# The norm behind w_o moves onto scores and expert blocks, and picks of four heads are decoded between router heads

## Chip, cores, metric

The kernel runs on one core of a Trainium2 chip. The metric is the device time of one execution in microseconds (us); the time before is the median of three runs.

## The reference, cut to what matters

Two transformer blocks follow each other. The change lies in the second, between its mixing output and its mixture of experts (256 tokens, width 2048, 8 heads, 128 keys per half, 16 picks of 16384 experts per head):

```python
x = x + mixed @ w_o[l]
x = x + peer(rmsnorm(x, norm_ffn_g[l]), peer_wq[l], keys1, keys2, peer_u[l], peer_v[l])

def peer(x, wq, keys1, keys2, u, v):
    q = (xf @ wq).reshape(t, PEER_HEADS, PEER_QDIM)
    s1 = jnp.einsum('thd,kd->thk', q[..., :half], keys1)
    s2 = jnp.einsum('thd,kd->thk', q[..., half:], keys2)
    v1, i1 = lax.top_k(s1, 16)
    v2, i2 = lax.top_k(s2, 16)
    cand_s = (v1[..., :, None] + v2[..., None, :]).reshape(t, PEER_HEADS, -1)
    top_s, pos = lax.top_k(cand_s, 16)
    expert = ...                                # from i1, i2 and pos
    gate = softmax(top_s)
    z = xc . u[expert]
    out = (gelu(z) * gate) @ v[expert]
```

rmsnorm divides each token's row by its root mean square and multiplies column k by a gain.

## The kernel before, in words

The kernel streams all weights once from memory, in units of 128x1024 floats (512 KB) through a ring of four slots of `raw`; SyncE (SP) loads slot n again as soon as DVE's split of it is done (`lo_ready`). A unit is split in two reduced-precision parts: ScalarE (ACT) writes `w_hi` (`split_hi`, L495), VectorE (DVE) `w_lo = raw - w_hi` (`split_lo`, L504). `ahead(...)` in an engine's program is such a split for the pair of units two pairs further on; it waits until TensorE (PE) has finished the unit four before. Activations are split likewise into `act_hi` and `act_lo`. Every engine's program is written out by hand in the order in which it runs; semaphores join them.

In `w_o`, PE runs blocks of 96 matmuls (`mix_block`, `tokens_out`, L601 to L603) for 512 columns of both halves of 128 tokens; DVE adds the banks to X (`add_blocks`), ACT squares the sum (`block_squares`). Then comes the norm: DVE adds the last bank (`add_last`, L1937), ACT squares and takes the root, DVE the reciprocal; X is scaled to XN (L1953, L1115), PE transposes it (`turn_ffn`, L2590, 32 of 128x128), ACT and DVE keep `act_hi` (`keep_ffn_hi`, L1121) and `act_lo` (`keep_ffn_lo`, L1959), 16 chunks of 128x256 each.

The router stage has 8 turns, one a head, of four blocks each: two query blocks and two expert blocks (`u`, the first 16 of 128). A block is two units of `halves_out`: 8 matmuls of 512 columns with `w_hi` (L561) and 8 of 256 with `w_lo` (L568). GpSimd (POOL) adds the two halves of a block that ACT copied (`add_copied`, L729). PE forms scores (L2620), ACT keeps them (`keep_scores`, L1160), DVE takes the top 16 of each half (`top16`, L1985 to L1993) and of the 256 candidates (L2011). In a turn DVE runs: splits of pair 0, of pair 1, top 16, of pair 2, top 16, of pair 3, candidates. ACT puts expert blocks through gelu and stores them (`save_early`).

In the decode stage PE goes on with 16 expert blocks in banks 2 and 3 (`decode_turn`; it waits for the addition two blocks back), ACT keeps the low half (`low_half`, L574), DVE adds the other (`add_halves`, L579), ACT puts gelu in place and stores the block (L1195, L1197). Between them DVE decodes the picks of all 8 heads: conversion of positions (L2040 to L2045), then for two index sets and two halves of the heads a comparison with 0 to 15 (L2053), a product with the indices (L2062) and a reduction (L2067); `more()` puts a weight split and, each second time, an addition in between. Then 80 blocks follow in which the gate table is built and scattered, 16 late blocks, and the product with `v`.

## Time and profile before

| | us |
|---|---|
| median of three runs (2696.03 to 2696.39) | 2696.3 |
| the profiled execution | 2696.89 |
| span of its trace | 2695.2 |
| PE busy | 2669.4 |
| DVE busy | 1835.3 |
| ACT busy | 1369.4 |
| POOL busy | 371.4 |

The span runs from the first to the last recorded instruction; the profiled execution's own time is 1.7 us longer. A busy PE is one with a matmul in flight, which is not PE at its peak: matmuls overlap, and a matmul of 512 columns that shows 0.39 us follows its forerunner after 0.23. In a timeline the number in front is the start, then the duration; what stands in brackets is the idle time of the engine before it and what ended it. Here PE has work for almost the whole span, so what matters is where it waits.

### The profile page before, as it was taken

To read this page: it belongs to the slowest core of one execution; us is meant where nothing else is said; L and a number is where in the kernel's file an instruction comes from. 1 tells how busy PE (TensorE), PEld (TensorE's weight loads), DVE (VectorE), ACT (ScalarE), POOL (GpSimd) and SP (SyncE) were. 2 spreads that over 40 slices of the span, in tenths; PEclk is the share of its full clock that TensorE was granted. 3 is DMA by queue.
4 is the path that set the end of the run, shared out by engine and by line. 5 is a ranking of instruction groups with operands and counts; after the bars stand their busy time and mean duration, and the time that the engine had idled before them with its cause. 6 is when DMAs were issued, how large, how long until landed. Compare 5 with 4: busy or idle time off the path is not lost.

```text
span 2695.2 us, 47112 instructions
## 1 busy us (share of the span) xinstructions
PE 2669.4 (99%) x14299; PEld 2298.4 (85%) x14299; DVE 1835.3 (68%) x2985; ACT 1369.4 (51%) x2066; POOL 371.4 (14%) x296
## 2 busy tenths in 40 slices
PE   8999999999999999999999999999999999999998
PEld 6888888898888998888888888888888888888887
DVE  6666665668987677489996777775565555555555
ACT  6454445555665444455455555554444444444444
POOL 0010000001011211011105555551000000000000
PEclk9999999999999999999999999999999999999999
DMA  7566555564554554655567777777976666666564
GB/s 257 189 216 213 181 199 177 177 219 159 172 176 156 167 168 157 195 201 186 195 201 212 202 202 203 201 204 218 305 240 217 217 217 219 212 220 216 200 241 156
DMA packets 204475, 543.26 MB, mean 202 GB/s; under 512 B 37504, under 2 KB 82816, under 8 KB 203392
## 3 DMA queue, kind: packets, MB, share of 16 engines
q1 hardware_dynamic: 148112, 486.74, 54.9%
q10 hardware_dynamic: 35568, 47.33, 5.0%
q0 software_dynamic: 20736, 8.46, 2.7%
q8 instruction: 30, 0.49, 0.1%
q14 instruction: 29, 0.24, 0.0%
HBM read 515.12 MB, written 27.33 MB: 201 GB/s over the span
## 4 chain that ended last, share of the span: by engine, by line
PE 94%; DVE 3%; ACT 1%; issue 1%; DMA 0%; SPq 0%; DVEq 0%; POOL 0%; ACTq 0%; POOLq 0%
PE bank L561 32%; PE bank L568 16%; PE bank L2693 8%; PE bank L2694 8%; PE bank L2695 8%; PE bank L601 4%; PE bank L603 4%; PE bank L602 4%; PE bank L2488 1%; DVE w_lo L504 1%; PE bank L527 1%; PE bank L528 1%; PE bank L529 1%; PE bank L2658 1%; PE bank L2465 0%
## 5 line engine op out<-in xcount | busy, mean ns | idle before, releaser
L504 DVE TENSOR_TENSOR w_lo<-raw,w_hi 128x1024 fp32r<-128x1024 f32 x902 | 1097.9, 1226 | 725.9 <-ACT w_hi L495 719.4
L495 ACT ACTIVATE w_hi<-raw 128x1024 fp32r<-128x1024 f32 x902 | 950.8, 1059 | 946.5 <-PE bank L568 363.1
L561 PE MATMUL bank<-act,w_hi 128*128 128x512 f32 x3840 | 975.2, 396 | 2.6 <-DVE cst L579 1.0
L561 PEld LDWEIGHTS bank<-act,w_hi 128*128 128x128 f32 x3840 | 692.0, 189 | 133.8 <-issue 6.4
L568 PEld LDWEIGHTS bank<-act,w_lo 128*128 128x128 f32 x3840 | 519.7, 190 | 33.1
L568 PE MATMUL bank<-act,w_lo 128*128 128x256 f32 x3840 | 535.6, 282 | 0.0
L2693 PE MATMUL bank<-w_hi,expert_act 128*128 128x512 f32 x1008 | 392.3, 389 | 0.1
L2694 PE MATMUL bank<-w_lo,expert_act 128*128 128x512 f32 x1008 | 392.2, 389 | 0.0
L2695 PE MATMUL bank<-w_hi,expert_act 128*128 128x512 f32 x1008 | 392.1, 389 | 0.0
L742 POOL DMA_INDIRECT g_kept<-slot_t x128 | 239.7, 1872 | 253.8 <-issue 170.4
L2693 PEld LDWEIGHTS bank<-w_hi,expert_act 128*128 128x128 f32 x1008 | 189.3, 188 | 39.6 <-DVE cst L579 0.5
L2695 PEld LDWEIGHTS bank<-w_hi,expert_act 128*128 128x128 f32 x1008 | 189.3, 188 | 39.3
L2694 PEld LDWEIGHTS bank<-w_lo,expert_act 128*128 128x128 f32 x1008 | 189.3, 188 | 39.1
L601 PE MATMUL bank<-w_hi,act 128*128 128x512 f32 x320 | 125.8, 393 | 2.0 <-DVE act L1401 1.1
L603 PE MATMUL bank<-w_hi,act 128*128 128x512 f32 x320 | 124.7, 390 | 0.0
L602 PE MATMUL bank<-w_lo,act 128*128 128x512 f32 x320 | 124.6, 389 | 0.0
L748 POOL TENSOR_TENSOR big<-big 128x1024 f32<-128x1024 f32 x2 | 5.8, 2878 | 839.4 <-DVE big L2196 839.4
L601 PEld LDWEIGHTS bank<-w_hi,act 128*128 128x128 f32 x320 | 60.1, 188 | 16.2 <-DVE w_lo L504 1.3
L603 PEld LDWEIGHTS bank<-w_hi,act 128*128 128x128 f32 x320 | 60.1, 188 | 12.6
L602 PEld LDWEIGHTS bank<-w_lo,act 128*128 128x128 f32 x320 | 60.1, 188 | 12.1
L729 POOL TENSOR_TENSOR big<-big 128x256 f32<-128x256 f32 x32 | 33.1, 1034 | 248.3 <-ACT big L1138 248.3
L2107 DVE SCALAR_TENSOR_TENSOR weighted<-cst,slot_t 128x256 fp32r<-128x256 f32 x128 | 61.3, 479 | 0.0
(344 smaller groups left out, 2498.4 us busy)
## 6 DMA issues: line engine op xcount, KB each, us to landing
raw<-in_stream SPq DMA_DIRECT2D x902, 512.0 KB
z_kept<-cst ACTq DMA_DIRECT2D x112, 128.0 KB, 2.4
cst<-z_kept ACTq DMA_DIRECT2D x112, 128.0 KB, 3.9
g_kept<-zeros POOLq DMA_DIRECT2D x16, 512.0 KB
big<-in_ukv ACTq DMA_DIRECT2D x16, 512.0 KB, 4.6
big<-g_kept SPq DMA_DIRECT2D x16, 512.0 KB, 5.6
big<-in_rows ACTq DMA_DIRECT2D x3, 1024.0 KB, 5.8
big<-in_x SPq DMA_DIRECT2D x2, 1024.0 KB, 10.2
```

Source lines behind the costliest of these rows:

```text
L495: act.activation(w_hi[:, s, :], raw[:, s, :], ACT.Copy).then_inc(hi_ready, 1)
L504: dve.tensor_tensor(w_lo[:, s, :], raw[:, s, :], w_hi[:, s, :].bitcast(F32), ALU.subtract).then_inc(lo_ready, 1)
L561: pe.matmul(bank[:, :], w_hi[:, s, kk * P:(kk + 1) * P], act2[:, k, :, :].rearrange("p a n -> p (a n)"), start=(k == 0), stop=False)
L568: mm = pe.matmul(bank[:, 0:S], w_lo[:, s, kk * P:(kk + 1) * P], act_hi[:, k, :], start=False, stop=(k == KT - 1))
L601: pe.matmul(outs[t], a_hi, hi, start=(k == 0), stop=False)
L602: pe.matmul(outs[t], a_hi, lo, start=False, stop=False)
L603: mm = pe.matmul(outs[t], a_lo, hi, start=False, stop=(k == KT - 1))
L742: pool.indirect_dma_start(g_kept, bass.IndirectOffsetOnAxis(ap=SLOT_INDEX[:, i:i + 1], axis=0), SLOT_GATE[:, i:i + 1], None, compute_op=AL ...
L2107: dve.scalar_tensor_tensor(out=weighted[:, tile, :, :], in0=iota.unsqueeze(1).broadcast_to([P, 2, P]), scalar=first_index[:, bass.ds(tok, 1)],
L2693: pe.matmul(o, a_hi, hi, start=first, stop=False, skip_group_check=True)
L2694: pe.matmul(o, a_hi, lo, start=False, stop=False, skip_group_check=True)
L2695: mm = pe.matmul(o, a_lo, hi, start=False, stop=False, skip_group_check=True)
```

## The change

It has three parts.

1. The norm. X goes untouched to the transposes. `turn_block` (the helper of the two earlier norms) transposes columns of blocks 0, 1, 2 in the middle of the next block of `w_o`, and of block 3 between the two units of the first query block. `keep_hi_tiles` and `keep_lo_tiles` make the tiles with the gain alone. The factor 1/rms of a token is put on later: on scores by `keep_scores` (two activations, a scale each); on expert blocks by a product with FFN_ROW, a row of 1/rms in all partitions, which PE makes of a matrix of ones and two diagonals. POOL multiplies the router stage's expert blocks, DVE all others (`scale_rows`), in front of gelu.
2. The picks of heads 0 to 3 are decoded in turns 2 to 7 of the router, two heads in three turns: one piece behind pair 0's splits, one behind pair 3's. In the decode stage heads 4 to 7 are left.
3. In the decode stage gelu writes to `Z_HALVES` instead of in place, and the wait for the store before last stands in front of gelu, no longer in front of the copy of the low half; the copy comes ahead of the gelu of the block before. The softmax's Exp comes after two turns, not four.

```diff
+            def early_block(n, block):
+                z = Z_HALVES[:, n, 0:S]
+                pool.wait_ge(copied, block + 5)
+                step(pool.tensor_tensor(z, z, Z_HALVES[:, n, S:2 * S], ALU.add))
+                pool.wait_ge(row_kept, 2)
+                step.wait()
+                pool.tensor_tensor(z, z, FFN_ROW, ALU.mult).then_inc(pool_summed, 1)
...
+            ahead(split_hi, act, "w_o", 0, 8, 15, units=(0,))
+            keep_hi_tiles(3, pa("ffn_gain"), act_hi, 3)
             ahead(split_hi, act, "w_o", 0, 8, 15, units=(1,))
-            keep_ffn_hi(range(8, 16))
...
-                    act.activation(PS[:, a, :, :].rearrange("p t n -> p (t n)"), banks[4 + a][:, 0:S],
-                                   ACT.Copy).then_inc(ps_kept[a], 1)
+                    for t in range(TT):
+                        kept = act.activation(PS[:, a, t, :], banks[4 + a][:, t * P:(t + 1) * P], ACT.Copy,
+                                              scale=rstd[:, t:t + 1])
+                    kept.then_inc(ps_kept[a], 1)
...
+            def save_decoded(i, n, last=False):
+                act.wait_ge(z_scaled, i * 2 + (n + 1))
+                act.wait_ge(z_saved[n % 2], i * 16 + (16 * (PH + n // 2) + 1))
+                dest = GZ[:, n % 2, :] if last else Z_HALVES[:, n % 2, 0:S]
+                act.activation(dest, GZ[:, n % 2, :], ACT.Gelu).then_inc(gelu_ready[n % 2], 1)
...
+                        if part == "w_o" and b and k == 1:
+                            keep_lo_tiles(4, pa("ffn_gain"), act_hi, act_lo, b - 1)
...
             add_last(0)
             mean_last(0)
             root_last(0)
-            dve.wait_ge(added[1], 8)
-            norm_last(0, 0)
             add_last(1)
-            for cc in range(1, 4):
-                norm_last(0, cc)
             mean_last(1)
             root_last(1)
-            dve.wait_ge(added[1], 9)
-            norm_last(1, 0)
-            norm_last(1, 1)
-            keep_ffn_lo(range(8))
             ahead(split_lo, dve, "w_o", 0, 8, 15, units=(0,))
-            keep_ffn_lo(range(8, 16))
+            keep_lo_tiles(4, pa("ffn_gain"), act_hi, act_lo, 3)
+            step(dve.memset(ONES, 1.0))
+            for t in range(TT):
+                step(dve.tensor_scalar(RSTD_DIAG[:, t, :], ident, rstd[:, t:t + 1], None, ALU.mult))
...
+            def early_picks(h, first):
+                lo = 2 * ((h - 2) // 3)
+                piece = 2 * ((h - 2) % 3) + (0 if first else 1)
+                a = piece // 3
+                if piece == 0:
+                    convert_picks(lo, lo + 2)
+                if piece % 3 == 0:
+                    compare_picks(a, lo, lo + 2)
+                elif piece % 3 == 1:
+                    step.wait()
+                    for head in range(lo, lo + 2):
+                        index_picks(a, head)
+                else:
+                    collect_picks(a, lo, lo + 2)
...
+            def scale_rows(n, block):
+                wait_summed(dve, block)
+                dve.tensor_tensor(GZ[:, n, :], GZ[:, n, :], FFN_ROW, ALU.mult).then_inc(z_scaled, 1)
...
-            mix_block(0, 1)
+            mix_block(0, 1, range(4))
+            turn_block(2, 0, added, 4)
+            mix_block(0, 1, range(4, 8))
...
+            def first_queries():
+                pe.wait_ge(copied, 1)
+                pe.wait_ge(added[1], 8)
+                pe.wait_ge(act_lo_ready, 4 * KT + 12)
+                halves_out(pe, pair_of("wqu", 0, 4, 0), odd_of("wqu", 0), banks[0], units=(0,))
+                turn_block(2, 3, added, 4)
+                halves_out(pe, pair_of("wqu", 0, 4, 0), odd_of("wqu", 0), banks[0], units=(1,), paced=4 * KT)
```

The order on DVE at the end of `w_o`, before (L1937 addition, L1941 to L1948 mean and reciprocal, L1953 scaling of X, L1959 `act_lo`, L504 weight split):

```order
L1937 TENSOR_TENSOR big<-big,bank 128x512
L1941 TENSOR_REDUCE stat<-stat 128x1
L1943 TENSOR_SCALAR stat<-stat 128x1
L1948 RECIPROCAL stat<-stat 128x1
L1953 TENSOR_SCALAR big<-big,stat 128x512
L1937 TENSOR_TENSOR big<-big,bank 128x512
L1953 TENSOR_SCALAR big<-big,stat 128x512 x3
L1941 TENSOR_REDUCE stat<-stat 128x1
L1943 TENSOR_SCALAR stat<-stat 128x1
L1948 RECIPROCAL stat<-stat 128x1
L1953 TENSOR_SCALAR big<-big,stat 128x512 x2
L1959 SCALAR_TENSOR_TENSOR act<-bank,par,act 128x256 x8
```

And now (line numbers of the changed kernel; L1941 addition, L1366 `act_lo`, L505 weight split):

```order
L1941 TENSOR_TENSOR big<-big,bank 128x512
L1945 TENSOR_REDUCE stat<-stat 128x1
L1947 TENSOR_SCALAR stat<-stat 128x1
L1952 RECIPROCAL stat<-stat 128x1
L1941 TENSOR_TENSOR big<-big,bank 128x512
L1945 TENSOR_REDUCE stat<-stat 128x1
L1947 TENSOR_SCALAR stat<-stat 128x1
L1952 RECIPROCAL stat<-stat 128x1
L505 TENSOR_TENSOR w_lo<-raw,w_hi 128x1024
L1366 SCALAR_TENSOR_TENSOR act<-bank,par,act 128x256 x4
L1964 MEMSET big 128x128
L1966 TENSOR_SCALAR big<-cst,stat 128x128 x2
```

The six scalings of X are gone, twelve of the sixteen `act_lo` tiles stand earlier in `w_o`, and the diagonals are new.

DVE in the router between turns 2 and 3, before (one of two candidate rounds, then the splits):

```order
L2011 TENSOR_TENSOR big<-big 128x256
L1985 MAX big<-big 128x8
L1987 MAX_INDEX big<-big 128x8
L1989 MATCH_REPLACE big<-big 128x256
L1991 MAX big<-big 128x8
L1993 MAX_INDEX big<-big 128x8
L504 TENSOR_TENSOR w_lo<-raw,w_hi 128x1024 x4
```

And now, with L2013 the reduction of `collect_picks`:

```order
L2051 TENSOR_TENSOR big<-big 128x256
L1974 MAX big<-big 128x8
L1976 MAX_INDEX big<-big 128x8
L1978 MATCH_REPLACE big<-big 128x256
L1980 MAX big<-big 128x8
L1982 MAX_INDEX big<-big 128x8
L505 TENSOR_TENSOR w_lo<-raw,w_hi 128x1024 x2
L2013 TENSOR_REDUCE big<-big 128x64
L505 TENSOR_TENSOR w_lo<-raw,w_hi 128x1024 x2
```

A piece of the decoding has come between the splits of pair 0 and pair 1; another one stands behind pair 3's splits, ahead of the next candidates.

PE at the start of the router, now (L2617 to L2619 end of `w_o`, L559 and L566 the two halves of a unit, L2287 transposes, L2652 the row of 1/rms, L2642 scores); before, all 32 transposes stood ahead of the first unit:

```order
L2619 MATMUL bank<-w_hi,mix_lo 128x512
L559 MATMUL bank<-act,w_hi 128x512 x8
L566 MATMUL bank<-act,w_lo 128x256 x8
L2287 MATMUL bank<-cst,big 128x128 x8
L559 MATMUL bank<-act,w_hi 128x512 x8
L566 MATMUL bank<-act,w_lo 128x256 x8
L559 MATMUL bank<-act,w_hi 128x512 x8
L566 MATMUL bank<-act,w_lo 128x256 x8
L559 MATMUL bank<-act,w_hi 128x512 x8
L566 MATMUL bank<-act,w_lo 128x256 x8
L2652 MATMUL bank<-big 128x128 x2
L2642 MATMUL bank<-big 128x128 x2
```

Only the last 8 transposes are left here, behind the first unit.

## Rows read from the trace of the kernel before

**Rows 1.** The page's busy line, then two stages: span, busy us of each engine, clock, DMA

```profile
PE 2669.4 (99%) x14299; PEld 2298.4 (85%) x14299; DVE 1835.3 (68%) x2985; ACT 1369.4 (51%) x2066; POOL 371.4 (14%) x296
...
1184.00:1361.00 177.00, 176.71 (x1032) 155.92 (x1031) 160.38 (x437) 90.66 (x124) 29.20 (x29) 1.00 0.57 188
1420.00:1880.00 460.00, 460.00 (x2676) 406.48 (x2675) 319.74 (x559) 242.76 (x388) 236.61 (x127) 1.00 0.74 205
```

**Rows 2.** Timeline of PE, end of w_o and start of the router's second block

```profile
1151.92 0.39 PE L2582 MATMUL bank<-w_hi,mix_lo 128*128 128x512 f32 x1
...
1166.20 2.00 PE L561 MATMUL bank<-act,w_hi 128*128 128x512 f32 x8
...
1169.00 2.00 PE L561 MATMUL bank<-act,w_hi 128*128 128x512 f32 x8
```

**Rows 3.** Timeline of PE, third decode block

```profile
1358.26 2.10 PE L561 MATMUL bank<-act,w_hi 128*128 128x512 f32 x8 [0.29 <-DVE cst L579]
```

**Rows 4.** Timeline of PE, transposes among matmuls in the stage of w_out

```profile
378.44 1.03 PE L2256 MATMUL bank<-cst,big 128*128 128x128 f32 x8
...
379.55 0.40 PE L602 MATMUL bank<-w_lo,act 128*128 128x512 f32 x1
```

**Rows 5.** Timeline of DVE and ACT at the end of w_o

```profile
1149.69 0.69 DVE L1937 TENSOR_TENSOR big<-big,bank 128x512 f32<-128x512 f32 x1 [0.41 <-PE bank L2582]
...
1151.66 1.04 ACT L495 ACTIVATE w_hi<-raw 128x1024 fp32r<-128x1024 f32 x1
...
1155.99 1.57 ACT L1121 ACTIVATE act<-bank,par 128x256 fp32r<-128x256 f32 x4 [0.30 <-PE bank L2590]
...
1156.87 1.66 DVE L1959 SCALAR_TENSOR_TENSOR act<-bank,par,act 128x256 fp32r<-128x256 f32 x4 [1.01 <-ACT act L1121]
```

**Rows 6.** Timeline of PE in the router, scores and the unit behind them

```profile
1334.56 0.61 PE L2620 MATMUL bank<-big 128*128 128x128 f32 x4
1334.93 2.09 PE L561 MATMUL bank<-act,w_hi 128*128 128x512 f32 x8
1336.86 0.99 PE L568 MATMUL bank<-act,w_lo 128*128 128x256 f32 x7
```

**Rows 7.** Timeline of DVE in the router, weight splits

```profile
1295.39 1.23 DVE L504 TENSOR_TENSOR w_lo<-raw,w_hi 128x1024 fp32r<-128x1024 f32 x1 [0.26 <-ACT w_hi L495]
...
1331.51 3.48 DVE L504 TENSOR_TENSOR w_lo<-raw,w_hi 128x1024 fp32r<-128x1024 f32 x3
1335.86 1.23 DVE L504 TENSOR_TENSOR w_lo<-raw,w_hi 128x1024 fp32r<-128x1024 f32 x1 [0.87 <-ACT w_hi L495]
```

**Rows 8.** Timeline of DVE at the start of decoding, and PE's fourth decode block

```profile
1357.70 0.42 DVE L579 TENSOR_TENSOR cst<-cst,bank 128x256 f32<-128x256 f32 x1
...
1359.24 2.40 DVE L504 TENSOR_TENSOR w_lo<-raw,w_hi 128x1024 fp32r<-128x1024 f32 x2
1361.56 0.41 DVE L579 TENSOR_TENSOR cst<-cst,bank 128x256 f32<-128x256 f32 x1
1361.89 2.28 DVE L2053 TENSOR_TENSOR big<-big,cst 128x2048 f32<-128x2048 f32 x1
...
1365.23 1.29 DVE L2062 TENSOR_TENSOR big<-big 128x512 f32<-128x512 f32 x2
...
1367.57 0.41 DVE L579 TENSOR_TENSOR cst<-cst,bank 128x256 f32<-128x256 f32 x1
...
1363.95 2.00 PE L561 MATMUL bank<-act,w_hi 128*128 128x512 f32 x8
```

**Rows 9.** Timeline of ACT in the loop behind the softmax's Exp

```profile
1396.22 1.28 ACT L495 ACT_TABLE_LOAD   x1
1397.51 1.06 ACT L495 ACTIVATE w_hi<-raw 128x1024 fp32r<-128x1024 f32 x1
```

**Rows 10.** By line, 1184 to 1361 us: duration ns min/median/max, first and last start

```profile
L504 DVE TENSOR_TENSOR w_lo<-raw,w_hi x62: 1203/1218/1227, 1183.8 to 1360.4; 128x1024 fp32r<-128x1024 f32 x62
L729 POOL TENSOR_TENSOR big<-big x29: 737/744/1297, 1188.1 to 1349.6; 128x256 f32<-128x256 f32 x29
```

More of the change, by code:

```diff
@@ L1168, in router_turn @@
                 keep_query(1)
+                if first:
+                    act.wait_ge(row_made, 2)
+                    act.activation(FFN_ROW, banks[6][:, 0:S], ACT.Copy).then_inc(row_kept, 1)
+                    act.wait_ge(rstd_ready, 7)
                 keep_scores(0)
@@ L1183, in early_turn @@
                     ahead(split_hi, act, "u_decode", i, 2, n, units=(0,))
+                    act.wait_ge(unit_done, 2 * pair_of("u_decode", i, 2, n) + 2)
+                    if first:
+                        act.wait_ge(z_saved[n], 16 * PH + 1)
+                    act.wait_ge(gelu_ready[n], i + (PH + 1))
+                    low_half(act, GZ[:, n, :], banks[2 + n])
+                    ahead(split_hi, act, "u_decode", i, 2, n, units=(1,))
                     if first and not n:
@@ L1228, in gates_turn @@
                     if gates:
+                        if first and not n:
+                            act.wait_ge(z_saved[0], 32 * PH + 1)
                         act.wait_ge(hot_used[2 * n + 1], i + 2)
@@ L1993, in top16, with convert_picks @@
                 return dve.max_index(idx[:, 8:16], vals[:, 8:16], work)
+            wide = TT * PK
+            def convert_picks(lo, hi):
+                cols = slice(lo * wide, hi * wide)
+                step.wait()
+                places = CP[:, lo:hi, :, :].rearrange("p h t k -> p (h t k)")
+                step(dve.tensor_scalar(CAU[:, 0, cols], places, 4, None, ALU.logical_shift_right))
+                step(dve.tensor_scalar(CAU[:, 1, cols], places, 15, None, ALU.bitwise_and))
+                step(dve.tensor_copy(I12F[:, lo:hi, :, :, :].rearrange("p h a t k -> p (h a t k)"),
+                                     I12[:, lo:hi, :, :, :].rearrange("p h a t k -> p (h a t k)")))
+                step.wait()
+                step(dve.tensor_copy(CA[:, :, cols], CAU[:, :, cols]))
@@ new lines, in compare_picks @@
+            def compare_picks(a, lo, hi):
+                step.wait()
+                step(dve.tensor_tensor(EQ[:, lo * wide * PK:hi * wide * PK].rearrange("p (n j) -> p n j", j=PK),
+                                       CA[:, a, lo * wide:hi * wide].unsqueeze(2)
+                                       .broadcast_to([P, (hi - lo) * wide, PK]),
+                                       iota[:, 0:PK].unsqueeze(1).broadcast_to([P, (hi - lo) * wide, PK]),
+                                       ALU.is_equal))
@@ L2023, in next_low @@
                     add_halves(dve, GZ[:, pair % 2, :], banks[2 + pair % 2], block_of("u_decode", 0, 2, pair))
+                    if not pair:
+                        dve.wait_ge(row_kept, 2)
+                    scale_rows(pair % 2, block_of("u_decode", 0, 2, pair))
             def more(count=1):
@@ L2037, in _ @@
             more(2)
[L2039 to L2045 removed]
+            half = PH // 2
@@ L2046, in _ @@
+            convert_picks(half, PH)
             more(2)
[L2047 to L2049 removed]
             for a in range(2):
[L2051 to L2070 removed]
@@ L2071, in _ @@
+                compare_picks(a, half, PH)
+                more()
+                step.wait()
+                for h in range(half, PH):
+                    index_picks(a, h)
+                    if h % 2:
+                        more()
+                collect_picks(a, half, PH)
+                more()
             dve.wait_ge(pick_exp, 1)
@@ L2624, in query_scores @@
                     halves_out(pe, pair_of("wqu", h, 4, 2 + a), odd_of("wqu", a), banks[2 + a])
-            queries_out(0, 0, paced=True)
+            first_queries()
             queries_out(0, 1)
+            pe.wait_ge(rstd_ready, 8)
+            for t in range(TT):
+                ins = pe.matmul(banks[6][:, t * P:(t + 1) * P], ONES, RSTD_DIAG[:, t, :], start=True, stop=True)
+            ins.then_inc(row_made, 1)
             pe.wait_ge(table_ready, 32)
```

149 lines of the change are left out of this document (44 added, 105 removed).

## Prediction, made blind

> **What bounds the kernel now.** I read the page first. TensorE (PE) is busy for 2669.4 us of the 2695.2 us span [rows 1], so a change can win only where PE waits, and can lose wherever a helper engine makes it wait. What to look for is therefore the few places where PE stands, and how near VectorE (DVE) is to being late elsewhere.
>
> The table by stage shows the second thing. In the router stage (1184 to 1361 us) PE has 176.71 of 177 us, and DVE 160.38: 91% [rows 1]. In the stage of the gate tables (1420 to 1880 us) DVE has 319.74 of 460 us, so it has room there.
>
> PE's timeline shows the first. The last w_o matmul starts at 1151.92; with 0.23 us each PE is through at 1152.15. The second router block starts at 1166.20 and a unit of sixteen matmuls lasts 2.80 us [rows 2]. So the first router block, two units or 5.60 us of work, took 14.05 us: **8.45 us** are the norm (32 transposes, square root, scaling) and its waits.
>
> The other place is where decoding starts: PE's third decode block begins at 1358.26 after a wait for DVE's addition (L579) [rows 3]. That addition frees the bank, and in DVE's program it stands behind all weight splits (L504, w_lo) and all of the top-16 work before it. So at this point DVE is already the bound: what DVE is late by here, PE is late by too.
>
> **The change, part by part.**
>
> *The norm leaves the path.* Raw X is transposed inside w_o: 8 transposes start at 378.44 and the matmul after next at 379.55 [rows 4]; less one matmul of 0.23 that is 0.88 us for 8. 24 of them in w_o: 2.64 us on PE. Then the first router unit runs at once (2.80), then the last 8 transposes (0.88) and four matmuls of the second unit (0.92): 4.60 us after the w_o end, which I call T. Chunk 12 needs the tiles that ACT and DVE write. From the start of DVE's addition to ACT's first weight split are 1.97 us, 1149.69 to 1151.66 [rows 5]. The first half's matmuls end twelve matmuls before 1152.15, at 1149.42, and its addition starts 0.27 later; so for the second half the addition starts at T+0.27 and ACT at T+2.24. The split (1.04) ends at T+3.3, when the first transposed chunks are there too; ACT's four tiles (1.57, [rows 5]) follow it, DVE's split ends at T+4.5, and DVE's four tiles (1.66, [rows 5]) make the last at T+6.1. Then one matmul (0.23) and the low half (0.95): T+7.3. Against 14.05 that is 14.05 - 7.3 - 2.64 = 4.1 us less. The row of 1/rms (two small products, the form of L2620) costs 0.37 start to start and makes the next group 0.09 longer [rows 6], so 0.45. **Front: -3.65 us.** Bounds: if nothing waited, 8.45 - 3.52 - 0.45 = -4.5; with 0.8 us of handovers more, -2.9. The tiles of blocks 0 to 2 (12 x 0.4 us on ACT and on DVE) fall into w_o, whose blocks last 22 us; nothing for them.
>
> *Picks between router heads.* DVE gets, in turns 2 to 7, twice: a conversion, and for each of two index sets a comparison and a reduction 128x1024 and two products 128x512. DVE instructions overlap by 0.08: three splits of 1.22 take 3.48 [rows 7], 1.13 each. Comparison and reduction I take at 1.13 (same width as the split; the 2048-wide one is 2.28, twice that, [rows 8]), two products at 1.20 (1.29 less 0.08, [rows 8]). The conversion took 1.20 us for four heads' widths and more (1357.70 to 1359.24, less the addition's 0.33, [rows 8]); a quarter of the width, between 0.3 and 1.2, I take 0.7. Sum: 2 x (0.7 + 2 x 3.46) = 15.2 us in six turns.
>
> What DVE can give: it waits for ACT's w_hi once 0.87 and twice 0.26 us a turn [rows 7]; with the lost overlaps 3 x 0.08 that is 1.63 us, 9.8 in six turns. The rest is lateness: 1.4, 2.0, 2.7, 4.1, 4.7 us at the ends of turns 2 to 6 and **5.4 us** at the end of turn 7. Until turn 6 it is covered by the ring of four weight units: the tightest split ends at 1332.74 and PE uses it at 1336.86 [rows 6, 7], 4.1 us later. At the end all of it meets the addition that PE already waits for. **Router: +5.4 us**; bounds +4.6 (conversion 0.3) and +7.1 (conversion 1.2, no overlap at half of the pieces).
>
> *Decoding.* DVE's cycle from addition to addition is 6.01 us where picks are decoded, 1361.56 to 1367.57 [rows 8], against PE's 5.59. Before, eight such blocks lose 8 x 0.42, less 1.97 of lead (addition done 1361.98, PE starts 1363.95, [rows 8]): 1.4 us. Now four blocks are left, each with a scaling of 0.45 (0.41 as L579, behind it on the same data): 4 x 0.87 - 1.83 = 1.65. **+0.25 us.** The gelu's own tile only takes ACT's wait for the z store off a copy that DVE does not wait for here; nothing.
>
> *ACT's tables.* The loop behind the softmax's Exp loads two tables a turn; it now has five turns, not three. A load takes 1.28 us and the next instruction follows at once [rows 9]. ACT's turn is then 4 splits of 1.04, 2 loads of 1.28 and six copies, gelus and DMA issues of some 0.4 each, about 9.2 of PE's 11.2 us: hidden. The Trainium skill, "ScalarE: Activation LUTs", "What ACT_TABLE_LOAD costs", adds a drain of 1380 ns to each switch. By it ACT would need about 12 us a turn and five turns would lose some 4 us, an estimate by that page. The rows show no such drain, so the sum leaves it out.
>
> *Scores and later blocks.* Two activations for one in keep_scores (some 0.2 us of ACT, half idle); POOL's 16 products of 0.74 us, hidden while the router's z tiles wait a turn anyway; DVE's 0.45 us on each of some 80 gate blocks and 16 late ones. 460 us hold 79 blocks [rows 1], so DVE goes from 70% to 77%; the scaling stands where DVE waits for w_hi. Nothing; if that cover were gone, each block would cost 0.45 us, 43 us in all, but a quarter of the stage is free.
>
> **Sum:** -3.65 + 5.4 + 0.25 = +2.0 us, on the profiled execution's own 2696.89 us: 2698.9. The median of the runs shown is 0.6 us lower, so 2698.3 us.
>
> **The rivals.**
>
> *A, the lateness stays hidden, faster.* If DVE's pieces are paid by its waits and by the ring, the router costs 0 and PE's first wait at 1358.26 (0.29 idle, 0.45 with the lost overlap) goes too: 2696.3 - 3.65 - 0.45 + 0.25 = 2692.4. For it: the ring's 4.1 us. Against it: the addition has no ring behind it. Half-way, at 2695.5, it shades into the forecast.
>
> *B, DVE is held by POOL, slower.* Before, POOL's sums last 0.74 or, when they meet a split, up to 1.30 us, while 62 splits keep to 1.203 to 1.227 [rows 10]: POOL gives way. Now POOL multiplies right behind its sum, at 12 new times in turns 2 to 7, and DVE is on two-input work then. If POOL came first each time and DVE stood for 0.74 us, that is 8.9 us on top, 2707; at half of them 2702.7. It decides from the fifth such meeting on (3.4 us), since only then is 0.2% passed. The Trainium skill, "SBUF — State Buffer", "Who interferes with whom", says that a DVE instruction with two SBUF inputs and a GpSimd one that reads SBUF exclude each other, and that the first to issue holds the ports. The trace agrees for the one order it shows; the other order it does not show.
>
> *C, the front gives less.* If ACT's or DVE's first tiles are late by a split each (2.2 us), 2700.5.
>
> **How the numbers follow.** Forecast 0.66, A 0.2, B 0.07, C 0.07. The forecast's own bounds: -4.5 + 4.6 and -2.9 + 7.1 on 2696.55 give 2696.6 to 2700.8. The range reaches to A and most of C: 2692.0 to 2701.5. A measurement can tell about 0.2%, 5.4 us, from no change. Faster than 2690.9 needs all of A and 1.5 us more: 0.05. Slower than 2701.7 is B and the forecast's tail: 0.1. The rest, 0.85, is within.
>
> **What would show it.** In the new profile: no stretch of PE waits of 1 us between w_o and the router, the second router block at about T+7.3; 24 transposes among the w_o matmuls; DVE's waits for w_hi gone from turns 3 to 7; a PE wait for DVE's w_lo or L579's like of several us in the last turn or at the third decode block. Wrong would be: DVE waits that stay in turns 5 to 7 (then A), splits longer than 1.23 us (then B), or PE idle in the gate stage.

## The result, and the profile after

The changed kernel takes **2710.4 us** (median of 6 runs, 2707.3 to 2712.2) against 2696.35 us before (also the median of 6, in which one run of 3301.9 us has no weight): ratio 1.0051, 95% interval 1.0038 to 1.0064. It is slower by 14 us, where 2698.3 us, 2 us slower, was forecast. Its profiled execution took 2712.0 us with a span of 2710.3 us, 15.1 us above the span before.

The waits of PE behind w_o come first (columns: who waited, in which line, for whom; us in all, times, longest). In the changed kernel's lines, L505 is the split that was L504, L577 the addition that was L579, L559 and L566 are the two kinds of matmul of a unit, L1196 is the decoded block's gelu.

```profile
PE bank L566 <- DVE w_lo L505: 6.0, 4, 1.9
PE bank L559 <- DVE cst L577: 5.6, 1, 5.6
PE bank L559 <- ACT big L1196: 1.8, 1, 1.8
PE bank L559 <- DVE act L1366: 0.3, 1, 0.3
```

The front went as forecast: the 8.45 us of norm and waits between w_o and the router [rows 2] are gone. What is new are four waits for w_lo in the router, one of 5.6 us at the third decode block [rows 3], and one of 1.8 us for a gelu. PE's timeline shows the first of the router units, the second router block at 1162.18, and then the third decode block:

```profile
1154.68 1.98 PE L559 MATMUL bank<-act,w_hi 128*128 128x512 f32 x8
...
1157.45 1.03 PE L2287 MATMUL bank<-cst,big 128*128 128x128 f32 x8
...
1162.18 2.00 PE L559 MATMUL bank<-act,w_hi 128*128 128x512 f32 x8
...
1311.46 2.09 PE L559 MATMUL bank<-act,w_hi 128*128 128x512 f32 x8
1315.42 1.25 PE L566 MATMUL bank<-act,w_lo 128*128 128x256 f32 x8 [1.87 <-DVE w_lo L505]
1316.48 3.58 PE L559 MATMUL bank<-act,w_hi 128*128 128x512 f32 x8
...
1368.56 3.77 PE L559 MATMUL bank<-act,w_hi 128*128 128x512 f32 x8 [5.59 <-DVE cst L577]
1372.13 1.91 PE L566 MATMUL bank<-act,w_lo 128*128 128x256 f32 x8
1373.84 2.34 PE L559 MATMUL bank<-act,w_hi 128*128 128x512 f32 x8
```

Eight matmuls that take 2.00 us took 3.58 and 3.77 us behind the two longest stalls. The table by stage says why (columns as in [rows 1]; the clock is the figure ahead of the DMA share): it fell to 0.50 of full speed, the lower of its two levels, 1.2 for 2.4 GHz.

```profile
1184.00:1361.00 177.00, 171.04 (x986) 149.62 (x985) 169.50 (x433) 88.70 (x132) 43.85 (x44) 0.99 0.56 179
1362.00:1368.00 6.00, 0.97 (x9) 0.76 (x7) 5.76 (x14) 1.33 (x2) 0.00 (x0) 0.97 0.09 35
1368.00:1374.00 6.00, 5.44 (x17) 4.67 (x18) 5.83 (x12) 0.42 (x1) 0.00 (x0) 0.50 0.91 246
1374.00:1380.00 6.00, 6.00 (x34) 5.22 (x33) 4.90 (x6) 2.69 (x4) 0.00 (x0) 0.96 0.65 234
```

PE had 176.71 of 177 us in the router stage [rows 1] and now has 171.04. DVE went from 160.38 to 169.50, and its waits for ACT's w_hi are all but gone: from 1206 to 1358 us they were 8.4 us before (last column: idle ahead of the splits, and for whom) and are 0.3 us now (the same row stands under run 2):

```profile
L504 DVE TENSOR_TENSOR w_lo<-raw,w_hi 128x1024 fp32r<-128x1024 f32 x52 | 62.2, 1217 | 8.6 <-ACT w_hi L495 8.4
```

The splits say what the forecast missed. They kept to 1.203 to 1.227 us [rows 10]; now the longest lasts 1.766 us (count, then minimum, median, maximum in ns):

```profile
L505 DVE TENSOR_TENSOR w_lo<-raw,w_hi x56: 1203/1218/1766, 1188.8 to 1357.1; 128x1024 fp32r<-128x1024 f32 x56
```

One such place, DVE and POOL side by side in the second turn (L732 is POOL's sum, L735 its new multiplication):

```profile
1222.03 2.88 DVE L505 TENSOR_TENSOR w_lo<-raw,w_hi 128x1024 fp32r<-128x1024 f32 x2
...
1228.26 2.34 DVE L505 TENSOR_TENSOR w_lo<-raw,w_hi 128x1024 fp32r<-128x1024 f32 x2
...
1222.59 1.25 POOL L732 TENSOR_TENSOR big<-big 128x256 f32<-128x256 f32 x1 [4.98 <-ACT big L1129]
1223.91 1.61 POOL L735 TENSOR_TENSOR big<-big,par 128x256 f32<-128x256 f32 x1
```

Two splits back to back take 2.34 us; with a POOL sum that came in the middle of the first they take 2.88. POOL waited for the first split to end and then went ahead of the second, which stood for 0.54 us. Before, the same sum met a split too (1.29 us for 0.74, [rows 10]). That place in the trace of before, at 1226.16 for 1222.59, DVE and then POOL:

```profile
1224.15 1.21 DVE L504 TENSOR_TENSOR w_lo<-raw,w_hi 128x1024 fp32r<-128x1024 f32 x1
1225.63 1.23 DVE L504 TENSOR_TENSOR w_lo<-raw,w_hi 128x1024 fp32r<-128x1024 f32 x1 [0.27 <-ACT w_hi L495]
1226.77 0.29 DVE L1985 MAX8 big<-big 128x8 f32<-128x128 f32 x1
...
1226.16 1.29 POOL L729 TENSOR_TENSOR big<-big 128x256 f32<-128x256 f32 x1 [4.75 <-ACT big L1138]
```

The sum fell into the second split of a pair, and behind that DVE was at a search, which reads one tile and kept its length. Two of a turn's sums met a split in this way in every turn from 1184 us on, 14 of the 29 in all, and each time it was the second split of a pair. My reading, which the runs below test: DVE's waits for w_hi (0.27 us here, 0.87 at the pair before) kept it in step with ACT, and ACT is what POOL waits for. **The new pieces use those waits up; with them goes the step, and the same POOL instructions fall between two splits.**

From pairs of the same matmuls in the two traces the 15.1 us come together so, to 0.1 us (the forecast's term beside it):

| part | measured | forecast |
|---|---|---|
| front: a router unit at 1192.25 now at 1188.68 | -3.6 | -3.65 |
| router and third decode block, stalls: 10.3 us later, plus 3.6 | +13.9 | +5.4 |
| rest of decoding, 1363.95 to 1424.44 now 1376.98 to 1436.04 | -1.4 | +0.25 |
| border of decode and gates: one block waits for a gelu | +2.0 | 0 |
| units at the lower clock behind the stalls of 5.6 and 1.8 us (2.7, 1.6) | +4.3 | 0 |

A third fall of the clock, behind the stall of 1.87 us in the router, cost PE 1.6 us too. It lies inside the 13.9 us and adds nothing to them: PE would have waited that much longer at the third decode block, where DVE sets the time.

### The profile page after: what moved, and what is told of

Same layout as the page of the kernel before. It is cut to its first block, busy times and chain, and to the rows that moved or that the text cites. A ratio compares the mean times of both kernels' runs of the same rounds, so it can differ in the third digit from the quotient of the medians.

```text
span 2710.3 us, 47380 instructions
## 1 busy us (share of the span) xinstructions
PE 2675.1 (99%) x14303; PEld 2303.8 (85%) x14303; DVE 1883.9 (70%) x3106; ACT 1376.1 (51%) x2085; POOL 381.2 (14%) x312
## 4 chain that ended last, share of the span: by engine, by line
PE 89%; DVE 7%; issue 2%; ACT 1%; DMA 0%; DVEq 0%; SPq 0%; POOL 0%; ACTq 0%; POOLq 0%
PE bank L559 29%; PE bank L566 15%; PE bank L2719 8%; PE bank L2720 8%; PE bank L2721 8%; PE bank L599 4%; PE bank L601 4%; PE bank L600 4%; DVE w_lo L505 2%; PE bank L2519 1%; PE bank L528 1%; PE bank L529 1%; PE bank L530 1%; PE bank L2684 1%; DVE big L1976 0%
## 5 line engine op out<-in xcount | busy, mean ns | idle before, releaser
L505 DVE TENSOR_TENSOR w_lo<-raw,w_hi 128x1024 fp32r<-128x1024 f32 x902 | 1102.4, 1233 | 690.8 <-ACT w_hi L496 684.0
L559 PE MATMUL bank<-act,w_hi 128*128 128x512 f32 x3840 | 979.1, 397 | 9.2 <-DVE cst L577 5.6
L559 PEld LDWEIGHTS bank<-act,w_hi 128*128 128x128 f32 x3840 | 695.0, 190 | 140.2 <-issue 10.0
L566 PEld LDWEIGHTS bank<-act,w_lo 128*128 128x128 f32 x3840 | 521.0, 191 | 40.8 <-DVE w_lo L505 7.7
L566 PE MATMUL bank<-act,w_lo 128*128 128x256 f32 x3840 | 537.4, 283 | 6.0 <-DVE w_lo L505 6.0
L749 POOL DMA_INDIRECT g_kept<-slot_t x128 | 233.5, 1825 | 240.0 <-issue 171.7
L601 PEld LDWEIGHTS bank<-w_hi,act 128*128 128x128 f32 x320 | 60.1, 188 | 12.7
L600 PEld LDWEIGHTS bank<-w_lo,act 128*128 128x128 f32 x320 | 60.1, 188 | 12.1
L2179 DVE TENSOR_TENSOR expert_act<-big,expert_act 128x256 fp32r<-128x256 f32 x128 | 53.7, 420 | 0.8 <-ACT expert_act L1264 0.8
```

Source lines behind the costliest of these rows:

```text
L505: dve.tensor_tensor(w_lo[:, s, :], raw[:, s, :], w_hi[:, s, :].bitcast(F32), ALU.subtract).then_inc(lo_ready, 1)
L559: pe.matmul(bank[:, :], w_hi[:, s, kk * P:(kk + 1) * P], act2[:, k, :, :].rearrange("p a n -> p (a n)"), start=(k == 0), stop=False)
L566: mm = pe.matmul(bank[:, 0:S], w_lo[:, s, kk * P:(kk + 1) * P], act_hi[:, k, :], start=False, stop=(k == KT - 1))
L600: pe.matmul(outs[t], a_hi, lo, start=False, stop=False)
L601: mm = pe.matmul(outs[t], a_lo, hi, start=False, stop=(k == KT - 1))
L749: pool.indirect_dma_start(g_kept, bass.IndirectOffsetOnAxis(ap=SLOT_INDEX[:, i:i + 1], axis=0), SLOT_GATE[:, i:i + 1], None, compute_op=AL ...
```

## The experiments

Theory H (held): what DVE is late by is its own new work and, on top, the time in which POOL's instructions hold it. Rival W: the work alone, the stretching being no cause. Two more questions go beside it: where the 1.8 us for a gelu come from, and whether the clock falls because of the stalls.

To compare runs I use the stretch from the first router unit to the third decode block on PE's timeline: 213.88 us in the changed kernel. It doesn't hang on small shifts ahead of it (with the norm moved the first router unit lay between 1153.92 and 1156.45 in the profiles). The stretching of DVE is, over 1206 to 1358 us, the mean of each kind of two-input instruction less its mean with POOL idle, times the count; in the changed kernel splits 49 x 0.123, products 8 x 0.133, candidate sums 12 x 0.064, comparisons 4 x 0.134: 8.4 us.

**1. POOL without its multiplications** (those 16 z blocks are left unscaled).

```diff
-                step(pool.tensor_tensor(z, z, Z_HALVES[:, n, S:2 * S], ALU.add))
-                pool.wait_ge(row_kept, 2)
-                step.wait()
-                pool.tensor_tensor(z, z, FFN_ROW, ALU.mult).then_inc(pool_summed, 1)
+                pool.tensor_tensor(z, z, Z_HALVES[:, n, S:2 * S], ALU.add).then_inc(pool_summed, 1)
```

> The changed kernel, but POOL only adds the two halves of the router's z blocks; the multiplication by the row of 1/rms behind each sum is left out, so those 16 blocks are not scaled. Theory H (held): of VectorE's lateness some 8.9 us, the sum of what 17 of its instructions take above their usual length, are time in which POOL's instructions hold it, most of them the new multiplications. Then most splits keep to 1.20 to 1.23 us, TensorE's four waits for w_lo (1.2 to 1.9 us) go, the wait at the third decode block falls from 5.6 to some 3 to 5 us, and the time is 2699 to 2704 us. Theory W (work): VectorE is late by its new pieces and lost waits alone, and stretched splits are only a record. Then the waits for w_lo stay and the time is 2709 to 2711 us.

Measured: 2707.1 us, between the two. Three waits for w_lo stayed, and half of the stretching (4.3 us): the sums, which never stretched a split before, do now. The stretch is 209.6 us (1156.45 to 1366.05), 4.3 less for 4.1 us less stretching. That fits H, but isn't the clean cut that I had expected, since I had put the stretching down to the multiplications.

**2. POOL idle in the router** (sums and multiplications left out; the scores take half of the queries).

```diff
-                pool.tensor_tensor(dest, halves[:, 0:S], halves[:, S:2 * S], ALU.add).then_inc(pool_summed, 1)
+                pool.sem_inc(pool_summed, 1)
...
```

> The changed kernel with POOL idle in the router: it only passes the signals on, so neither the halves of the queries and of the z blocks are added nor the z blocks scaled (the scores take the first halves). Theory H+W: the first run took away the multiplications, and of 8.9 us of stretched VectorE instructions 3.7 were left, by sums that still met it. Now all stretching goes. What stays is VectorE's own work, 15.5 us of new pieces less the 9.8 us it can give: at most one wait for w_lo, and 4.5 to 5.5 us at the third decode block counted from the last w_o matmul against 12.3 in the changed kernel (stalls of the router and this one together). Time 2700 to 2704 us. Theory W (the stretching is a record only, the rest of the lateness is something unseen): 2706 us or more.

Measured: 2702.3 us (ratio 1.0019, 1.0010 to 1.0029). By kind of instruction, 1206 to 1358 us (columns: count, busy us, mean ns, idle ahead of it), first of the changed kernel:

```profile
L505 DVE TENSOR_TENSOR w_lo<-raw,w_hi 128x1024 fp32r<-128x1024 f32 x49 | 63.6, 1337 | 0.3 <-ACT w_hi L496 0.3
L2008 DVE TENSOR_TENSOR big<-big 128x512 f32<-128x512 f32 x8 | 6.2, 819 | 0.0
```

and with POOL idle:

```profile
L505 DVE TENSOR_TENSOR w_lo<-raw,w_hi 128x1024 fp32r<-128x1024 f32 x50 | 58.7, 1214 | 0.3 <-ACT w_hi L496 0.3
L2003 DVE TENSOR_TENSOR big<-big 128x512 f32<-128x512 f32 x8 | 5.2, 686 | 0.0
```

PE's waits with POOL idle, to 1420 us:

```profile
PE bank L559 <- DVE cst L577: 4.9, 1, 4.9
PE bank L566 <- DVE w_lo L505: 0.3, 1, 0.3
```

No instruction is stretched, DVE still waits for w_hi only 0.3 us, and the stretch is 205.3 us (1154.62 to 1359.93): 8.6 us less, the 8.4 of stretching. This settles H against W: the stretching is a cause.

**3. All picks back in the decode stage**, POOL multiplying as in the changed kernel.

```diff
-                if h >= 2:
-                    early_picks(h, True)
...
-                if h >= 2:
-                    early_picks(h, False)
...
+                for low in (0, half):
+                    compare_picks(a, low, low + half)
```

> The changed kernel with all heads decoded in the decode stage, as before; the norm stays moved, and POOL multiplies in the router. Theory H: VectorE still waits for w_hi in the router, 1.63 us a turn, so two to four holds of 0.53 us a turn are hidden, TensorE has no wait in the router, and what is left is the front (-3.6), eight decode blocks instead of four at 0.87 us each less the lead of 1.83 (5.1 against 1.4 before, +3.7) and the wait at the border of decode and gates with its clock (+3.6): 2700.1 us, 2698 to 2702. Theory W gives the same here. If the holds by themselves make TensorE wait, there are waits for w_lo in the router and the time is 2704 us or more.

Measured: 2699.4 us. In the router DVE has its waits for w_hi back, and POOL's 16 multiplications cost nothing:

```profile
L505 DVE TENSOR_TENSOR w_lo<-raw,w_hi 128x1024 fp32r<-128x1024 f32 x52 | 62.1, 1216 | 8.4 <-ACT w_hi L496 8.4
```

PE's waits in the same run:

```profile
PE bank L559 <- DVE cst L577: 4.2, 8, 0.6
PE bank L559 <- ACT big L1196: 1.8, 1, 1.8
```

The stretch is 200.0 us, with PE's waits for w_lo at nothing. So DVE's own work for four heads' picks makes 205.3 - 200.0 = **5.3 us**, the forecast's 5.4; POOL's holding makes the rest.

**4. The picks alone in the kernel before**, norm, scalings and gelu as they were.

> The kernel before with one part of the change: picks of heads 0 to 3 are decoded between the router heads (and the exponential moved to where the shorter decode stage wants it). The norm, the scalings and the gelu are as before, so POOL makes sums only. Theory H+W: as in the run without the multiplications, sums that meet a VectorE without gaps hold it, some seven times 0.54 us, on top of 5.3 us of its own work: the third decode block starts 9 to 10 us later than before, the clock falls behind that stall (2 us), the later decode blocks lose 1.4 us less, no wait at the border: 2704 to 2708 us. Theory M: only a product right behind a sum holds VectorE, the sums alone never do, as in the kernel before: then 5.3 us and the time is 2700 to 2702.5 us.

Measured: 2707.3 us. From the second router block (1166.20 before, 1166.10 here) to the third decode block it takes 202.1 us against 192.1: 10.1 us more, for 5.3 of work and 4.6 us of stretching by sums alone (50 splits at a mean of 1277 ns make 3.2 of it). Theory M falls: a plain sum holds DVE as a product does, once DVE is out of step. The norm has no part in this loss.

**5. POOL kept to the searches.** A search reads one tile. In a first run POOL waited for a signal that DVE gives ahead of a search, in a second for one that it gives when the search's first instruction has ended (the edit shown).

```diff
                 step(dve.max(vals[:, 0:8], work))
                 step.wait()
+                if tell:
+                    dve.sem_inc(softplus_ready, 1)
...
                 pool.wait_ge(copied, block + 5)
+                pool.wait_ge(softplus_ready, turn * 2 + (n + 4))
```

> The changed kernel, but POOL starts the sum and product of a router z block only when VectorE is at a top-16 search, whose instructions read one tile (one signal ahead of the second head half's search for the first block, one ahead of the candidates' search for the second). No work is left out. Theory H: the stretching by the z blocks goes, that by the two query sums a turn (two to four of 0.54 us) stays; the lateness at the third decode block is 5 to 7 us less than in the changed kernel and the time 2701 to 2705 us. If only what POOL asks for matters and not when, 2709 to 2712 us.

Measured: 2709.4 us, not what I expected. The signal ran ahead of the splits in front of it: a sum (L733) started its wait at 1248.32, with the first of two splits, and the pair took 2.89 us. One query sum came late as well, PE waited 0.5 us for it.

```profile
1248.27 2.89 DVE L505 TENSOR_TENSOR w_lo<-raw,w_hi 128x1024 fp32r<-128x1024 f32 x2
...
1248.32 1.76 POOL L733 TENSOR_TENSOR big<-big 128x256 f32<-128x256 f32 x1 [6.19 <-DVEq L2041]
```

> The changed kernel, but POOL starts a router z block's sum and product only when the first search instruction of a top-16 search has ended (the run that signalled ahead of the search had its signal sent while splits were still to run). Theory H: no z block then meets a split, only the query sums do (two to six times 0.54 us); the third decode block starts 207 to 209 us after the first router unit against 213.9 in the changed kernel and 205.3 with POOL idle; time 2702 to 2707 us. Rival: POOL's instructions hold VectorE whatever it does, also in a search: searches last longer by some 0.5 us each time and the time is 2709 us or more.

Measured: 2707.4 us, 0.4 above what was expected and below the rival's 2709. The z blocks meet no split any more and the searches keep their length (MAX8 of 256 at 428 ns as before), so POOL doesn't hold a search. Still the stretch is 210.6 us, more than the 207 to 209 expected. The rows say why:

```profile
L505 DVE TENSOR_TENSOR w_lo<-raw,w_hi 128x1024 fp32r<-128x1024 f32 x48 | 58.4, 1257 | 0.0
...
L2054 DVE TENSOR_TENSOR big<-big 128x256 f32<-128x256 f32 x12 | 6.2, 514 | 0.0
...
L1979 DVE MATCH_VALUE_LOAD big<-big 128x8 f32 x37 | 3.4, 92 | 2.7
```

Query sums still hold splits (2.1 us), POOL's product now runs into the second candidates' sum (12 x 0.1), and the signal costs DVE 1.4 us by itself (2.7 idle for 1.3). 5.3 + 3.8 + 1.4 is 10.5 us, and 10.6 was measured.

**6. Two heads instead of four**, one piece a turn, and PE's wait at the border changed as in 8.

```diff
-                lo = 2 * ((h - 2) // 3)
-                piece = 2 * ((h - 2) % 3) + (0 if first else 1)
+                a, piece = (h - 2) // 3, (h - 2) % 3
...
-            convert_picks(half, PH)
+            convert_picks(2, PH)
...
```

> Picks of heads 0 and 1 alone are decoded in the router (one piece a turn, 7.7 us in all, against 9.8 us that VectorE can give), heads 2 to 7 in the decode stage in two groups of three for each index set, and TensorE waits at the border of decode and gates for the sum, not the gelu. Theory H+W: VectorE is never late in the router, so POOL meets it in gaps and holds nothing; the front keeps its 3.6 us, VectorE has 7.3 us less to do in the decode stage than with all picks there, where the waits summed to 6 us, and the border costs 0.4. Time 2691 to 2694 us, faster than before. Rival: the row multiplications behind every sum are what decode pays for, and the waits for the addition stay at over 0.4 us a block: 2696 us or more.

Measured: 2703.1 us, ten above what I expected, and the most telling miss. Half of the work is gone from the router, and the stretching grew:

```profile
L505 DVE TENSOR_TENSOR w_lo<-raw,w_hi 128x1024 fp32r<-128x1024 f32 x49 | 64.4, 1357 | 1.1 <-ACT w_hi L496 1.1
```

PE's waits in the same run:

```profile
PE bank L559 <- DVE cst L577: 5.3, 1, 5.3
PE bank L566 <- DVE w_lo L505: 3.0, 3, 1.4
```

By the expectation 7.7 us of work against 9.8 us of gaps should have left 2.1 us over; the stretching, 10.2 us here, made it 8.1 late, and the stretch is 8.9 above that of run 3 (the working takes all waits as used up, and 1.1 us of them are left). The expectation treated DVE's waits as spare time; by these rows they were also what kept POOL from between the splits. One piece a turn uses up most of them (1.1 us are left of 8.4), each meeting then costs some 0.54 us, and that uses up the rest.

All router runs together, in us above run 3 (200.0):

| run | work | stretching | signal | sum | measured |
|---|---|---|---|---|---|
| changed kernel | 5.3 | 8.4 | | 13.7 | 13.9 |
| 1, sums only | 5.3 | 4.3 | | 9.6 | 9.6 |
| 2, POOL idle | 5.3 | 0 | | 5.3 | 5.3 |
| 4, picks alone | 5.3 | 4.6 | | 9.9 | 10.1 |
| 5, first signal | 5.3 | 6.0 | | 11.3 | 12.1 |
| 5, in the search | 5.3 | 3.8 | 1.4 | 10.5 | 10.6 |
| 6, two heads | -2.1 | 10.2 | | 8.1 | 8.9 |
| 8, border | 5.3 | 7.4 | | 12.7 | 12.8 |

The 5.3 is itself run 2's measurement. The -2.1 is the expectation's 7.7 less 9.8. (Run 8 has the changed kernel's router, and in its profile no fall of the clock there: it is shorter by what is less in stretching, not by 1.6 us more, so the fall in the changed kernel's router added nothing to what DVE is late by. Run 4's figure is the 10.1 us against the kernel before.)

**7. A version that beats both: the same decode work beside more blocks.** Run 3 lost 0.87 us in each of six blocks (38.78 us from 1371.58 to 1410.36, 33.54 without waits) and some 0.4 in two more, while the blocks behind them had DVE time over. All picks stay in decoding, a unit more behind each reduction, border as in 8 (the edit against run 3):

```diff
-                    collect_picks(a, low, low + half)
-                    more()
+                    collect_picks(a, low, low + half)
+                    more(2)
```

> All picks are decoded in the decode stage, with one more unit's split put behind each of its four reductions, so that the same VectorE work lies beside ten blocks instead of eight; the norm stays moved, POOL multiplies in the router, and TensorE waits at the border of decode and gates for the sum. Theory: the run with all picks there lost 6.2 us in eight blocks (3.57 us for 2.80 each) and 14 us later TensorE had to wait for nothing; per group VectorE has 7.1 us of pick work and gets 1.27 us a unit beside the splits, so five units a group leave 0.75 us a group, 3.0 us in all, 1.2 us behind the lead of 1.83. Border 0.4 instead of 2. Time 2699.4 - 5.0 - 1.6 = 2692.8 us (2691 to 2695), faster than before. Rival: the picks then come too late for their transposes ahead of the last decode turn, TensorE waits there, and the time is 2696 us or more.

Measured: **2693.6 us** (11 runs, 2693.05 to 2695.12; ratio to before 0.9991, 0.9982 to 1.0000), 16.8 us under the changed kernel and 2.7 under the kernel before. The gain over before is small and its interval ends at 1.0000; still, each of the 11 runs is faster than each of the 16 of the kernel before that were taken beside them (2695.77 us and more). The decode stage in the table by stage, columns as in [rows 1], first in run 3, where PE is short of 4.2 us:

```profile
1354.00:1424.00 70.00, 65.76 (x366) 56.61 (x366) 66.34 (x85) 45.35 (x58) 3.96 (x2) 1.00 0.63 201
```

then here, short of 0.9 us:

```profile
1354.00:1424.00 70.00, 69.08 (x391) 60.29 (x392) 68.45 (x87) 48.17 (x62) 0.99 (x1) 1.00 0.65 215
```

and PE's waits in this run from the router on:

```profile
PE bank L559 <- DVE cst L577: 1.1, 3, 0.6
PE bank L2681 <- DVE weighted L2132: 0.3, 1, 0.3
```

**8. The border: wait for the sum, not for the gelu**, all else as in the changed kernel.

```diff
                 for n in range(2):
-                    pe.wait_ge(gelu_ready[n], i + (2 * PH + 1))
+                    wait_summed(pe, block_of("u_gates", i, 2, n - 2))
```

> The changed kernel, but in the gate stage TensorE waits, ahead of a block, for the sum of the block two before it (both readers of the bank are through then) and no longer for its gelu. Theory G: the 1.82 us wait at the border comes from the gelu's new place behind the next block's copy and split, and the fall of the granted clock behind it (a unit of 4.45 us for 2.80) comes from that wait; both go, 3.6 us less, 2706.8 us (2705 to 2708). Rival: TensorE then waits there for the next split instead, and the time stays within 1 us of 2710.4.

Measured: 2707.4 us, 3.0 less than the changed kernel. The two kernels' runs overlap (2707.11 to 2708.74 here, 2707.34 to 2712.22 there), so the 3.0 us alone prove little; the trace shows the 1.8 us wait gone, and in its place are 0.35 us for the first gate tile:

```profile
PE bank L2684 <- DVE weighted L2135: 0.4, 1, 0.4
```

The change had moved the decoded gelu behind the next block's copy and split on ACT. Inside decoding nobody waits for it, but the gate stage's first block does, and by then ACT's order made it wait for PE's last decode unit. The place in the changed kernel:

```profile
1450.53 0.38 ACT L572 ACTIVATE cst<-bank 128x256 f32<-128x256 f32 x1 [1.67 <-PE bank L566]
1450.81 1.05 ACT L496 ACTIVATE w_hi<-raw 128x1024 fp32r<-128x1024 f32 x1
1451.76 0.41 ACT L1196 ACTIVATE big<-cst 128x256 f32<-128x256 f32 x1
...
1452.32 3.21 PE L559 MATMUL bank<-act,w_hi 128*128 128x512 f32 x8 [1.82 <-ACT big L1196]
```

**9. Stalls alone, in the kernel before.** PE waits at four places for POOL, which multiplies a tile 1, 2, 3 and 6 times.

```diff
+            def hold_pe(unit, length):
+                pool.wait_ge(unit_done, unit)
+                for _ in range(length):
+                    step(pool.tensor_tensor(idle_tile, idle_tile, idle_tile, ALU.mult))
+                    step.wait()
+                pool.sem_inc(warm_ready, 1)
```

> The kernel before, with four stalls of TensorE and nothing else: ahead of the last decode turn, of the gate stage's turns without tables, of the late blocks and of the experts it waits for POOL, which starts when all its work so far is done and multiplies a 128x256 tile 1, 2, 3 and 6 times one after the other (0.74 us each and more where it meets VectorE). Theory C: the granted clock falls because TensorE stood still, if it stood long enough, and each fall costs 1.6 to 2.8 us on top: stalls of about 1.1, 1.9, 2.8 and 5.3 us, none of it behind the first, behind the last one a unit that lasts over 4.4 us for 2.8; time 2709 to 2714 us. Rival: the falls in the changed kernel come from another thing (VectorE's or the DMA's load in the router); then the units behind all four stalls last what they did and the time is 2707 us, the stalls alone.

Measured (one execution): 2762.2 us, since the second stall became 51.6 us instead of 1.9: POOL was still at its scatters and came late. The stalls are of other lengths than planned, but the question is answered (starts and durations of PE's groups, with the wait ahead of them):

```profile
1427.72 2.11 PE L562 MATMUL bank<-act,w_hi 128*128 128x512 f32 x8 [0.54 <-POOLq L743]
...
1958.13 3.20 PE L562 MATMUL bank<-act,w_hi 128*128 128x512 f32 x8 [3.36 <-POOLq L743]
1961.13 1.60 PE L569 MATMUL bank<-act,w_lo 128*128 128x256 f32 x8
1962.58 2.01 PE L562 MATMUL bank<-act,w_hi 128*128 128x512 f32 x8
```

The stretch behind the third stall in the table by stage, columns as in [rows 1]:

```profile
1960.00:1962.00 2.00, 2.00 (x9) 1.71 (x8) 0.00 (x0) 0.00 (x0) 0.00 (x0) 0.50 1.07 351
```

A stall of 3.4 us, with DVE, ACT and POOL at nothing behind it, costs 1.55 us more, at a clock of 0.50, as in the changed kernel (the 16 matmuls took 4.45 us, and take 2.9 behind a stall without a fall). The DMA engines were busy there; in the kernel before they were just as busy at full clock:

```profile
1958.00:1960.00 2.00, 2.00 (x14) 1.84 (x13) 1.55 (x2) 0.59 (x2) 0.00 (x0) 1.00 1.13 338
```

The unit behind the 51.6 us stall took 4.22 us for 2.80; behind the 0.54 us nothing happened. So a stall is enough for a fall, without anything of what else ran in the router.

## Why the prediction was wrong, point by point

- **Front, -3.65 us: right.** Measured -3.6. The second router block started 7.5 us behind the last w_o matmul's slot (1162.18, w_o through at 1154.68), 7.3 forecast; the 24 transposes and the row of 1/rms cost what the sum says. With the norm moved, the first router unit lay between 1153.92 and 1156.45 us in the other profiles, so the tenths are those of this pair of traces.
- **DVE's own work, +5.4 us: right in size**, by run 2 against run 3 5.3 us. **The step that failed** is the one that takes this work for the whole lateness, in the paragraph "What DVE can give: it waits for ACT's w_hi". DVE was late by 13.9 us, not 5.4: 5.3 us of work and 8.4 us in which POOL held it. I spent those waits as spare time and read [rows 10] as "POOL gives way". POOL gives way only to the split under way; that it hurt nobody behind it was due to the very waits that I spent: with them (run 3) the splits' mean is 1216 ns, without them 1337.
- **Rival B, given 0.07, is what happened in kind**: DVE held by POOL, 8.4 us. Its chance was too low, and that its full price of 8.9 us comes so near is luck. It was 12 new multiplications at 0.74 us each; a meeting costs 0.54 us, which makes some 16 of them, and by runs 1 and 4 the old sums hold too (4.3 and 4.6 us), and by run 3 the multiplications hold nothing while DVE is in step. What decides is not what POOL got to do but DVE's place in time. "Splits longer than 1.23 us (then B)" was the right sign to look for. The prediction drew on the Trainium skill, "SBUF — State Buffer", "Who interferes with whom" (the first to issue holds the ports). These traces agree and show the order that it could not take from the rows: a POOL instruction that waits through one split is ahead of the next, and that one stands for 0.54 us of POOL's 0.74.
- **Headroom of the ring, 4.1 us: right in kind.** At 5.4 us of lateness it would have covered the router (run 2: one wait of 0.3 us). With the stretching it ran out in the third of the six turns with pieces (first wait for w_lo at 1265.21).
- **Decoding, +0.25 us: untested for four heads**, since PE comes so late to it that DVE catches up (-1.4). With all picks there (run 3) a block lost 0.87 us, as forecast.
- **"Nothing" for the gelu's own tile: wrong**, +2.0 us and a fall of the clock of 1.6 us (run 8 is 3.0 us faster without that wait). I asked who waits inside decoding and didn't follow the signal to its other reader, PE's first gate block.
- **Clock, no term: wrong by its absence**, 4.3 us. The rows of before show 1.00 throughout because nothing there stood long enough in these stages. The stall of 5.6 us costs 8.3.
- **ACT's tables, scores, later blocks: nothing, and nothing it was.** PE's distance to before is 15.2 us at the first gate tile (1458.60 for 1443.44) and 15.1 at the end, through some 74 scaled gate blocks. Five turns of two table loads cost PE nothing: between the third decode block and the border it waits for nobody. The drain of 1380 ns that the Trainium skill has in "ScalarE: Activation LUTs", "What ACT_TABLE_LOAD costs", doesn't show as such: the load at 1390.13 us starts 0.02 us behind the split ahead of it, and the gelu follows 1.29 us later. Four of the loads at the top of a turn have 1.05 us of idle time in front, in which the issue of a store (0.36 us) lies; what the rest of it is stays open.

The range ended at 2701.5 us. The forecast with the 8.4 us of stretching alone would have been 2706.7. What the range lacked was less the width of each term than that the meeting of two engines, the stall it makes and the clock behind the stall come together and all add.

## What to carry to other kernels

Waits of an engine that shares ports with another are not all spare time: they can be what keeps the two apart. Before filling them, look for the neighbour's instructions in the same stretch, and price each at what it would take between two back-to-back instructions (here 0.54 us). Price a stall of PE of 5 to 6 us at a third to a half more, for the clock (1.8 to 2.7 us here). And where work overloads one stretch of a stage, try first to spread it over the same stage: that was worth more here (5.8 us between runs 3 and 7, the border's share in it; moving the picks made the kernel slower) than moving it into a stage that looked 9% free.

## What the runs showed of the hardware

- Two-input instructions of DVE and POOL take turns: POOL's 128x256 (0.74 us alone) lasts up to 1.8 us with its wait for a split, and the next split then lasts 1.77 us for 1.22. Searches, which read one tile, keep their length beside it (run 5).
- DVE's signal to POOL, given between two instructions without a wait of its own, went out while the splits ahead of it were still to run (run 5); behind a wait for its own last result it was on time and cost DVE some 0.1 us each (1.4 us for the 13 of the stretch).
- The granted clock behind stalls, in the profiles of this case from the router on (16 matmuls, start to start): 19 stalls of 1.1 to 1.7 us had no slower unit behind them; of seven of 1.82 to 1.87 us five had one (4.45 us for 2.9); all eleven of 3.4 us and more had, for 1.3 to 2.7 us of extra time where whole units show it. The length of the stall isn't all that decides: the same 1.82 us stall at the border was followed by a unit of 4.45 us in the changed kernel and of 2.90 us in run 3, and far ahead of the router, at 24 us and 17 us behind PE's first matmul, a wait of 1.05 to 1.06 us that seven of the profiles have was followed by the clock of 0.50 in two of them (run 1 and the first of run 5: 4.8 us for 3.2; why in these two is open). The changed kernel's runs spread over 4.9 us, and their mean clocks go with the time, from 0.998 in the two fastest to 0.996 in the slowest; that this is the chance of a fall fits, but was not tried by itself.
